# First two layers of a four-layer model on one core: the heads' weighing put in pairs, the shared-key heads put in alternating halves, and one wait of a gate unit moved

## The reference

```python
h = rmsnorm(x, norm_mix)
proj = h @ w_in
points = np.cumsum(IN_SIZES)[:-1].tolist()
qa, ka, va, qb, kb, vb, qc, kc, vc, gates = jnp.split(proj, points, axis=-1)
...
o_a = swa_sink_attention(apply_rope(heads(qa, SWA_Q_HEADS), cos, sin),
                         apply_rope(heads(ka, SWA_KV_HEADS), cos, sin),
                         heads(va, SWA_KV_HEADS), sinks)
o_b = stick_breaking_attention(heads(qb, SB_HEADS), heads(kb, SB_HEADS), heads(vb, SB_HEADS))
o_c = moba_attention(apply_rope(heads(qc, MOBA_HEADS), cos, sin),
                     apply_rope(heads(kc, MOBA_HEADS), cos, sin),
                     heads(vc, MOBA_HEADS))
g = jax.nn.sigmoid(gates.reshape(B, S, N_BRANCHES, D_MODEL) + b_gate.reshape(N_BRANCHES, D_MODEL))
merged = (g[:, :, 0] * (o_a @ w_branch[0])
          + g[:, :, 1] * (o_b @ w_branch[1])
          + g[:, :, 2] * (o_c @ w_branch[2]))
x = x + merged @ w_out
```

## Time and profile before

| | before |
|---|---|
| median of 3 runs | 2624.29 us (2619.41 to 2630.31) |
| the profiled execution, its own time | 2628.95 us |
| its span | 2627.3 us |
| PE busy | 2494.2 us (95%) |
| DVE busy | 1844.2 us (70%) |
| ACT busy | 1453.8 us (55%) |
| mean DMA rate | 234 GB/s |
| granted TensorE clock, mean | 0.961 of full speed |

### The profile page before, as it was taken

One profiled execution on the slowest core, in us unless ns is written; L12 is line 12 of the kernel. 1 busy time (PEld: TensorE's weight loads), 2 busy tenths in 40 slices (PEclk: granted clock), 3 DMA queues, 4 the chain that ended last, 5 costly groups with the idle time before them and its releaser, 6 DMA issues.

```text
span 2627.3 us, 37563 instructions
## 1 busy us (share of the span) xinstructions
PE 2494.2 (95%) x13426; PEld 2097.0 (80%) x13426; DVE 1844.2 (70%) x2063; ACT 1453.8 (55%) x1446; POOL 62.1 (2%) x75
## 2 busy tenths in 40 slices
PE   8998999999999999999999998999999999999995
PEld 7876899897679998868998767878777777878784
DVE  3665687656657876645445647888888888888886
ACT  5554444455534444533343435777777777777773
POOL 0100000000000000000000001000000000000000
PEclk9998999999999999779999878999999999999997
DMA  6433455443344554427553325999999999999996
GB/s 262 141 132 129 176 180 187 150 156 120 136 157 181 192 187 153 152 82 217 198 191 129 112 80 223 382 354 373 355 372 354 364 364 356 378 351 365 362 367 254
DMA packets 93854, 615.78 MB, mean 234 GB/s; under 512 B 9776, under 2 KB 17600, under 8 KB 22464
## 3 DMA queue, kind: packets, MB, share of 16 engines
q1 hardware_dynamic: 88544, 591.51, 61.1%
q0 software_dynamic: 5216, 23.04, 2.4%
HBM read 599.30 MB, written 15.20 MB: 234 GB/s over the span
## 4 chain that ended last, share of the span: by engine, by line
PE 60%; issue 25%; DVE 6%; ACT 4%; DVEq 3%; POOL 1%; ACTq 1%; DMA 0%; POOLq 0%
PE bank L307 18%; PE bank L309 17%; PE bank L308 17%; PE bank L393 3%; ACT w_hi L467 3%; DVE w_lo L561 3%; DVEq L553 2%; PE bank L418 1%; PE bank L403 1%; PE bank L1567 1%; POOL probs L735 1%; DVE probs L624 0%; DVE x_tok L1976 0%; PE bank L419 0%; PE bank L1450 0%
## 5 line engine op out<-in xcount | busy, mean ns | idle before, releaser
L561 DVE TENSOR_TENSOR w_lo<-raw,w_hi 128x2048 fp32r<-128x2048 f32 x550 | 1252.0, 2295 | 436.8 <-ACT w_hi L467 414.1
L467 ACT CAST w_hi<-raw 128x2048 fp32r<-128x2048 f32 x550 | 1049.8, 1913 | 472.2 <-PE bank L309 460.7
L307 PE MATMUL bank<-w_hi,hT_hi 128*128 128x512 f32 (+3 forms) x1360 | 542.9, 399 | 26.4 <-DVE w_lo L561 13.8
L309 PE MATMUL bank<-w_hi,hT_lo 128*128 128x512 f32 (+3 forms) x1360 | 527.8, 388 | 0.0
L308 PE MATMUL bank<-w_lo,hT_hi 128*128 128x512 f32 (+3 forms) x1360 | 527.4, 388 | 0.0
L307 PE MATMUL bank<-hT_hi,w_hi 128*128 128x256 f32 (+1 forms) x1568 | 449.4, 287 | 5.9 <-DVEq L579 5.6
L308 PE MATMUL bank<-hT_lo,w_hi 128*128 128x256 f32 (+1 forms) x1568 | 444.8, 284 | 0.0
L309 PE MATMUL bank<-hT_hi,w_lo 128*128 128x256 f32 (+1 forms) x1568 | 444.8, 284 | 0.0
L307 PE MATMUL bank<-w_hi,oT_hi 128*128 128x512 f32 x876 | 345.8, 395 | 17.7 <-DVE oT_lo L2151 11.1
L308 PE MATMUL bank<-w_lo,oT_hi 128*128 128x512 f32 x876 | 342.7, 391 | 0.0
L309 PE MATMUL bank<-w_hi,oT_lo 128*128 128x512 f32 x876 | 342.2, 391 | 0.0
(11 more groups left out here) (270 smaller groups left out, 1784.8 us busy)
## 6 DMA issues: line engine op xcount, KB each, us to landing
raw<-in_weights_dram SPq DMA_DIRECT2D x554, 1024.0 KB, 6.9
token_rows<-all_cols SPq DMA_DIRECT2D x11, 512.0 KB, 7.2
arena<-in_norms_dram POOLq DMA_DIRECT2D x2, 2048.0 KB, 8.4
nat<-token_rows POOLq DMA_DIRECT2D x8, 512.0 KB, 8.0
unit_rows<-probs POOLq DMA_DIRECT2D x8, 512.0 KB, 8.9
arena<-in_b_gate_dram POOLq DMA_DIRECT2D x6, 512.0 KB, 4.6
unit_rows<-all_cols SPq DMA_DIRECT2D x4, 512.0 KB, 9.2
tables<-in_tables_b_dram POOLq DMA_DIRECT2D x1, 1216.0 KB, 5.9
```

The costliest lines, as they stand in the source:

```text
L307: mm(out, st[0], mv[0], start=start, stop=False, skip_group_check=True)
L309: return mm(out, st[1], mv[0], start=False, stop=stop, skip_group_check=True)
L467: self.isa.copy(m.w_hi[:, slot, :], m.raw[:, raw, :]).then_inc(m.hi_ready, 1)
L561: self.isa.tensor_tensor(m.w_lo[:, slot, :], m.raw[:, raw, :], m.w_hi[:, slot, :].bitcast(F32), ALU.subtract).then_inc(m.lo_ready, 1)
```

## The change

`weigh_pair` does the weighing of two neighbouring heads, one after the other, with a wait for `pt_ready` before each. In `softmax_beside` PE now waits at odd h only for `pt_ready` of the head before (which also frees bank 2) and goes on to `turn_probs`; at even h it weighs heads h - 2 and h - 1, and after the loop 6 and 7. In branch b (`out`) `weigh_pair` takes the place of two calls of `weigh`. In branch a the heads are taken in the order 0, 4, 1, 5, 2, 6, 3, 7: step h works in half h % 2 of tile h // 2, and the rows of `w_branch[0]` and the sinks are put in the same order on the host. PE's wait for `oT_ready` moves from ahead of unit 4 to ahead of its fifth part, and DVE counts `oT_ready` ahead of `weigh_rows(1)`.

```diff
@@ -419,6 +419,21 @@
         self.isa.matmul(out[:, P:S], v[1], pt[:, S:S + P], start=False, stop=True,
                         skip_group_check=True).then_inc(m.weighed, 1)
 
+    def weigh_pair(self, h, v_of, b, first_known=False):
+
+        m = self.m
+        for i in range(2):
+            if i or not first_known:
+                self.eng.wait_ge(m.pt_ready, self.w.next(m.pt_ready))
+            if i == 0:
+                self.bank(b)
+            v = v_of(h + i)
+            pt = m.probsT[:, i, :]
+            out = m.bank[b][i * DH:(i + 1) * DH, 0:S]
+            self.isa.matmul(out, v[0], pt[:, 0:S], start=True, stop=False, skip_group_check=True)
+            self.isa.matmul(out[:, P:S], v[1], pt[:, S:S + P], start=False, stop=True,
+                            skip_group_check=True).then_inc(m.weighed, 1)
+
     def softmax_heads(self, parts_of, v_of, ident):
 
         for h in range(8):
@@ -442,13 +457,18 @@
         self.turn_probs(0, 2, ident)
         next(filler)
         for h in range(1, 8):
-            self.weigh(h - 1, v_of(h - 1), 2, (3, 3))
+            if h % 2:
+                self.eng.wait_ge(self.m.pt_ready, self.w.next(self.m.pt_ready))
+            else:
+                self.weigh_pair(h - 2, v_of, 3, True)
+            self.known.add(2)
             self.turn_probs(h % 4, 2, ident)
             if h in (1, 3):
                 self.scores(0, parts_of(h + 3))
                 self.scores(1, parts_of(h + 4))
             next(filler)
-        self.weigh(7, v_of(7), 2, (3, 3))
+        self.weigh_pair(6, v_of, 3, True)
+        self.known.add(2)
         next(filler)
 
 class Scalar(Engine):
@@ -777,9 +797,9 @@
 
         self.eng.wait_ge(m.roped, w.next(m.roped, 3))
         self.softmax_beside(
-            lambda h: [(a_tile(m, QA + h % 4)[(h // 4) * DH:(h // 4 + 1) * DH, :],
-                        a_tile(m, KA)[(h // 4) * DH:(h // 4 + 1) * DH, :])],
-            lambda h: [a_v(m, t, (h // 4) * DH, (h // 4 + 1) * DH) for t in range(TT)], ident,
+            lambda h: [(a_tile(m, QA + h // 2)[(h % 2) * DH:(h % 2 + 1) * DH, :],
+                        a_tile(m, KA)[(h % 2) * DH:(h % 2 + 1) * DH, :])],
+            lambda h: [a_v(m, t, (h % 2) * DH, (h % 2 + 1) * DH) for t in range(TT)], ident,
             itertools.chain(self.unit(2), self.unit(3)))
         self.eng.wait_ge(m.roped, w.next(m.roped, 4))
         self.eng.wait_ge(m.copied, w.next(m.copied, 2))
@@ -788,10 +808,10 @@
                         a_tile(m, KC + h // 2)[(h % 2) * DH:(h % 2 + 1) * DH, :])],
             lambda h: [a_v(m, t, P + 512 + h * DH, P + 512 + (h + 1) * DH) for t in range(TT)], ident,
             itertools.chain(self.unit(0), self.unit(1)))
-        self.eng.wait_ge(m.oT_ready, w.next(m.oT_ready))
         for u, base in ((4, 0), (5, 4)):
-            for _ in self.unit(u, base):
-                pass
+            for part, _ in enumerate(self.unit(u, base)):
+                if u == 4 and part == 3:
+                    self.eng.wait_ge(m.oT_ready, w.next(m.oT_ready))
         self.stay_warm(WARM // 3)
         self.eng.wait_ge(m.nat_ready, w.next(m.nat_ready))
         self.turn_rows(m.nat, (0, 1, 2, 3), ident)
@@ -844,7 +864,7 @@
                             skip_group_check=True).then_inc(m.to_dve[h % 4], 1)
 
         def out(h):
-            self.weigh(h, [a_v(m, t, P + h * DH, P + (h + 1) * DH) for t in range(TT)], None, (4, 4))
+            self.weigh_pair(h, lambda h: [a_v(m, t, P + h * DH, P + (h + 1) * DH) for t in range(TT)], 4)
 
         def rotation(job):
             _, tile, _ = job
@@ -863,13 +883,11 @@
         rotation(KVA)
         self.eng.wait_ge(m.copied, self.w.next(m.copied, 2))
         out(0)
-        out(1)
         logits(4)
         logits(5)
         self.inputs(QC1)
         rotation(QC0)
         out(2)
-        out(3)
         logits(6)
         logits(7)
         self.inputs(KC0)
@@ -880,8 +898,8 @@
             sums(h)
         self.inputs(VC)
         rotation(KC1)
-        for h in range(4, 8):
-            out(h)
+        out(4)
+        out(6)
 
     def unit(self, u, base=4):
 
@@ -1132,8 +1150,8 @@
         self.stick_beside_inputs(4, cos, sin)
         self.softmax_beside(0, m.tab(A_TABLES, "band"), sinks, (2, 3), None)
         self.softmax_beside(8, m.tab(A_TABLES, "causal"), None, (0, 1), 3)
+        self.eng.drain().then_inc(m.oT_ready, 1)
         self.weigh_rows(1)
-        self.eng.drain().then_inc(m.oT_ready, 1)
         for u, base in ((4, 0), (5, 4)):
             self.split(2)
             self.gate_in(u, base, 32 if u == 4 else 0)
@@ -2419,11 +2437,13 @@
     turned(qb), turned(kb), rows(vb)
     turned(paired)
     turned(np.concatenate([ka, va], 1))
+    heads_in_pairs = [np.concatenate([w_branch[0].reshape(8, DH, D)[[j // 2 + 4 * (j % 2) for j in range(8)]]
+                                      .reshape(512, D)]), w_branch[1], w_branch[2]]
     turned(qc), turned(kc), rows(vc)
     for u in (2, 3, 0, 1, 4, 5):
         i, h = u // 2, u % 2
         rows(w_in[:, o[9] + i * D + 512 * h:o[9] + i * D + 512 * h + 512])
-        rows(w_branch[i][:, 512 * h:512 * h + 512])
+        rows(heads_in_pairs[i][:, 512 * h:512 * h + 512])
     for a, b in ((0, 256), (256, 512), (512, 640), (640, 768), (768, 896), (896, 1024)):
         out.append(chunk_of(w_out[a:b]))
 
@@ -2446,7 +2466,8 @@
     taps = np.concatenate([conv_w, conv_b[None]], 0).reshape(4, 2, FF_SUBS, 2, P)
     return np.concatenate([
         norm_mix.reshape(KT, P).T, norm_ffn.reshape(KT, P).T,
-        taps.transpose(4, 2, 1, 3, 0).reshape(P, -1), np.broadcast_to(sinks, (P, 8))], 1)
+        taps.transpose(4, 2, 1, 3, 0).reshape(P, -1),
+        np.broadcast_to(sinks[[j // 2 + 4 * (j % 2) for j in range(8)]], (P, 8))], 1)
 
 
 def tables_b():
```

## The result

| | before | changed | ratio, 95% interval |
|---|---|---|---|
| median of 4 runs each | 2626.24 us | 2592.08 us (2582.98 to 2593.52) | 0.9854 [0.9836, 0.9873] |
| measured again, other rounds | 2631.09 us | 2591.42 us | 0.9840 [0.9823, 0.9857] |
| span of the profiled execution | 2627.3 us | 2591.9 us | |

By the first interval 33 to 43 us were saved, by the second 37.5 to 46.5. Ratios and intervals are taken over the single runs; the medians of the two rows lie 34.2 and 39.7 us apart. Forecast were 37.4 us and 2587 us, with 2576 to 2601 as the range. The measured median, 2592, lies nearer to the 2591 of the rival in which the slow clock stays than to 2587: the times alone can't tell the two apart, the traces can.

What follows compares the result with a forecast made beforehand. PE, busy for 95% of the span, was taken as the bound, with its own work or its holes to win. Terms of 5.1, 12.6, 3.3, 4.2 and 12.2 sum to 37.4 us off the 2624.3 us median: 2587 us, range 2576 to 2601.

Steps and rivals of the forecast that it cites:

- the rival in which the slow clock stays: Holes left in branch c still bring PE to 1.2 GHz, so the clock gain falls away: 2591 us; chance 0.15.
- A: Branch a's scores in alternate halves: each pair of heads takes 0.93 us in place of 1.57, saving 5.1 us.
- C: PE's holes at h = 3 of both softmaxes shrink, a new one comes at head 4 of branch c; 3.3 us saved.
- B: Weighing in pairs in both softmaxes: the second head is free, 0.79 us saved at each of 16 pairs, 12.6 us.
- D: Behind branch c's hole at h = 3 the clock stays at full speed, saving 4.2 us; the least sure term.
- PE at 0.5 behind h = 3: Sign of being wrong: PE running at half its full clock after the hole at h = 3.
- E: PE's wait for `oT_ready` ahead of unit 4 goes, and units 4 and 5 run at full clock: 12.2 us saved.
- No overlap: Rival: weighing in different column halves does not overlap, so the gain from pairs is lost: 2600 us; chance 0.07.
- the bound on DVE: Rival: shortened steps find DVE late, and gains return as waits for bank 3 and `probs_ready`: 2608 us; chance 0.06.
- the held pair: Rival: the pair's second head waits for `pt_ready`; at 4 us each 2651 us; chance 0.01 slower, 0.02 unchanged.

Runs made afterwards that it cites:

- a_only: The kernel before with only branch a's heads reordered, so that neighbours' scores lie in alternate halves; ratio 0.9996.
- late_alone: The changed kernel with each head weighed by itself one step later, no two side by side but heads 6 and 7; 2599.04 us, ratio 0.9895.
- no_e: The changed kernel with PE's wait for `oT_ready` and DVE's count back in their old places; 2605.0 us, ratio 0.9881.
- warm_fill: The kernel before with 12 matmuls of zeros by PE ahead of its unmoved wait for `oT_ready`; ratio 1.0007.
- gates_later: The changed kernel with ACT taking the first unit's sigmoids behind the third pair's exponentials, not ahead of the cast and copy; 2582.09 us, ratio 0.9822.
- b_only: The kernel before with only the pairs of weighing, heads in the old order and `oT_ready` in its old place; ratio 0.9912.
- e_only: The kernel before with only the wait for `oT_ready` moved; ratio 0.9970, run again with more rounds 0.9941.

## Why the prediction was right

**A, scores in halves: right.** 0.93 us for 1.57 in all eight pairs, 5.1 us of PE's time. As the text had it, C's hole in branch a is where part of it is lost. Without B that is 1.6 us, and 0.5 in new waits; what else a_only lacks is the clock's.

**B, pairs: right.** 0.80 to 0.81 us for two heads in 13 of the 16 pairs, 0.88 and twice 0.95 in the others: 12.3 us for 12.6. late_alone took the neighbour away from 12 pairs and lost 8.0 us; 12 x 0.79 = 9.5 less shorter holes were expected. With that the Trainium skill's rule on weight loads (TensorE: Matmul & The Clock Gate, part 3) is decided against for this shape: here, with both heads on all 128 rows and in different column halves, the second costs 0.01 us. But the prediction took only that one rule from the page. In a table of the same part of the Trainium skill three matmuls packed by columns, of 32 columns each, are 2.38 times as fast. So the skill does not speak against packing by columns as such, and the trace agrees with that table in kind.

**C, the holes: right in place, a little short in size.** 1.31, 1.52 and 0.94 against 1.1, 1.4 and 0.8. What was saved by them is 0.46 twice in branch a and 1.40 twice at h = 3 of branch c, less 0.94 at head 4 in the first layer, plus the second layer's 0.5, and less a wait that the text did not have, 0.23 us in each layer ahead of branch a's first part (for `oT_lo`, because the scores ahead of it are shorter): 2.8 us for 3.3. In the second layer the new hole at head 4 did not come, since the slow clock (D) brought PE there later; in no_e, where the clock stayed up, it is 0.94 in both layers.

**D, the clock in branch c: the size came out, the reason given did not.** The step that failed reads "with two holes of 1.4 and 0.8 I take it that the clock stays up, since 1.77 left it up". In the second layer it fell behind the hole of 1.52, two stretches of 6.5 us behind h = 3 in the two layers of the changed kernel:

```profile
201.44:207.94 6.50, 6.50 (x39) 4.75 (x40) 4.71 (x17) 6.21 (x14) 0.00 (x0) 1.00 0.42 161
...
677.69:684.19 6.50, 6.50 (x31) 4.66 (x31) 4.71 (x17) 5.45 (x12) 0.00 (x0) 0.74 0.43 165
```

PE's timeline there, the scores and the next pair in both layers:

```profile
201.91 0.93 PE L393 MATMUL bank<-arena 64*128 64x128 f32 x8
...
205.72 0.66 PE L433 MATMUL bank<-probsT,arena 128*64 128x256 f32 x4
...
678.16 0.93 PE L393 MATMUL bank<-arena 64*128 64x128 f32 x8
...
683.56 0.66 PE L433 MATMUL bank<-probsT,arena 128*64 128x256 f32 x4
```

The fall cost 683.56 - 678.16 = 5.40 us between the start of the scores and the next pair where the first layer took 205.72 - 201.91 = 3.81, so 1.6 of the 4.2 us; since PE then did not wait at head 4, the layer was only 0.5 us longer in the end (125.75 against 125.28). PE at 0.5 behind h = 3 was among the signs of being wrong that the prediction named, and it did show, in this one place. The ground "since 1.77 left it up" falls as well: in warm_fill the clock fell behind the same hole of 1.77 us (0.65). And in the second layer of the kernel before the clock had also been at 0.74 behind branch b's hole of 1.70 (from 627.46), which I had not looked at; its first two scores were 634.38 - 628.35 = 6.03 us apart, in the first layer 4.45. That 1.6 us was won back without being in the sum. The two errors cancel, by luck: 37.4 forecast, 38.0 in the stretch.

**E: right.** From the last weighing to the end of unit 5 PE took 277.27 - 234.34 = 42.9 and 772.99 - 730.74 = 42.3 us before, and 36.3 in both layers now: 12.5 us for 12.2. No chunk came late. Added up, the parts as measured give 5.1 + 12.3 + 2.8 + 4.2 + 12.5 = 36.9 us; where the last 1.1 us of the 38.0 lie is not shown.

**The rivals.** A clock that stays slow was half true in one layer. No overlap, the bound on DVE and the held pair are excluded by late_alone, by gates_later (in which PE, though it came earlier still, waited for DVE 0.4 us in the whole of a layer's two softmaxes) and by the rows of the pairs, in which no second head starts more than 0.1 us late.

## What to carry to other kernels

Two small matmuls that use different halves of the array (rows as in A, or columns as in B) should stand side by side in the program, even if one must be kept back a step for it; the price of that is read from places where the kernel does so already. Work that is saved ahead of a chain of other engines comes back as a longer wait at its end (part A alone: holes longer by 1.6 of its 5.1 us; none with the chain cut): look for the instruction in that chain which waits for something that nothing urgent needs, and put it behind. A move that needs no result yet can stand ahead of the wait, and the wait then costs nothing.

## What the runs showed of the clock

I had taken the fall of the granted clock for a matter of the hole's length. Counted over both layers of the fourteen traces, from branch b's last pairs to the end of unit 5, holes of PE of over 1 us and what the clock did in the 6.5 us behind (fallen: below 0.99):

| hole, us | holes | fallen |
|---|---|---|
| 1.02 to 1.50 | 15 | 0 |
| 1.51 to 1.53 | 9 | 2 |
| 1.70 to 1.78 | 34 | 5 |
| 2.57 to 2.96 | 12 | 8 |
| 4.02 to 4.06 | 8 | 8 |

Length sets how often, not whether. Many of these are one hole of the program seen in several kernels, so the shares are rough. What decides in the middle is open. The two kernels that were profiled twice (changed, e_only) fell behind the same holes both times, so at 677.69 and 678.39 the changed one, but not behind the hole of the same length in its first layer. That looks like a matter of the place. But behind branch b's hole of 1.70 us in the first layer, up to which the matmuls of all these kernels are the same, the clock fell in three of thirteen traces, and the time at which it comes does not sort them:

```profile
131.93:138.43 6.50, 6.50 (x27) 4.87 (x28) 4.33 (x15) 4.13 (x11) 0.59 (x1) 0.74 0.23 84
...
131.93:138.43 6.50, 6.50 (x35) 5.11 (x36) 4.33 (x15) 4.13 (x11) 0.58 (x1) 1.00 0.24 84
```

The first is b_only's, the second e_only's. So two executions can differ by such a fall without a change of the program as its cause. Its price at the step where it came was 1.5 to 3.2 us, less where PE then waited less further on. The 15.6 us of e_only are of this kind: 12.2 and two falls less. Its hole of 2.96 us at 210.35 left the clock at 1.00, where 2.92 at 210.40 had brought the kernel before to 0.54 (2.7 us), and branch b's in the second layer, at 618.92, left it up as well (1.6 us); new small holes at head 4 of branch c, 0.99 and 0.67, take 1.2 of it back. That makes 15.3. So a term for the clock is a chance times a price, and the sum of a change should carry it as that.
